# Issue order of the first transfers in a one-core hybrid decoder step: input tiles on two queues, parameters behind the first weight chunk

## The chip, the cores and the metric

The kernel runs on one core of a Trainium2 chip. The metric is the device time of one execution in microseconds (us); times of one kernel agree within a tenth of a us here. The core has a matmul engine (PE, TensorE, with its weight loads as PEld), VectorE (DVE), ScalarE (ACT), GpSimd (POOL) and a sync engine (SP), which only issues DMAs and waits. DMAs issued by SP go through one queue (q1 in the profile) and those issued by ACT through another (q10). Both are worked off by the same 16 DMA engines.

## What is computed

One decode step of one decoder layer for a prompt of 256 tokens and a sample group of 8 x 4 tokens, all f32, width 1024. The front of it, which is all that this case turns on:

```python
def rmsnorm(x, w):
    x32 = x.astype(jnp.float32)
    y = x32 * lax.rsqrt(jnp.mean(x32 * x32, axis=-1, keepdims=True) + EPS)
    return (y * w.astype(jnp.float32)).astype(x.dtype)
...
    xn = rmsnorm(x, norm1_w)
    proj = xn @ w_in
```

Behind it two branches (HGRN2 and RWKV-7) are run on the columns of `proj`, gated, merged and added to x; then comes a mixture of 32 experts, 4 for each token, whose weights (some 400 MB) are all read from memory; then a last RMSNorm. The small parameters of the RWKV-7 branch (`rwkv_mu`, `rwkv_w0`, `rwkv_a0`, `rwkv_k_k` and others) and of HGRN2 enter only after the first projection.

## The kernel before

The program is written out engine by engine, with semaphores; no scheduler reorders it, so the order of each engine's instructions is the order in the code.

**Start.** The 288 rows of x are three row tiles: tile 0 and tile 1 (128 rows of 4 KB each, 512 KB) of the prompt, tile 2 (32 rows) of the samples. SP issues, in this order: the norm weight (`norm1_w`, one row of 4 KB, into `norm_bc[0:1]`), the three row tiles into `xs`, the shift state (8 rows), chunk 0 of `w_in` (1 MB, as 1024 pieces of 1 KB), and four constants (`lora` twice, `g2`, `rb_bc`). Before chunk 1 it waits for `par_loaded`, that is, for all eleven parameter transfers; then it issues chunks 1 to 3, and each further chunk waits for PE to free its place in a ring of four.

ACT loads its function table, and issues the eleven parameter transfers: ten small ones into `par_rows` (14 or 4 rows of 512 B) and one of 128 rows (`gn_bc`). Then, for each row tile, it waits for `x_loaded{t}` and does a square with row sum (1.0 us), a logarithm and an exponential: that gives the tile's 1/rms (`rstd`).

PE waits for `ident` (POOL) and `norm_loaded`, and spreads the norm weight over 128 partitions by two matmuls of a row of ones with `norm_bc[0:1]`, into banks 6 and 7; their end is `par_T` 1. Then come `keep_busy(5)`, matmuls with no use for the result, and the transposes of the three tiles (8 each), each tile behind `xn_done`. `keep_busy(2)`, a wait for the five copies of the transposed tiles by ACT (`xT_evac`), and the projections follow: project(0) is the first matmul with chunk 0.

DVE waits for `par_T` 1, and for each tile for `rstd`; then it multiplies x by 1/rms and by the spread weight in banks 6 and 7, in two halves of 512 columns, and signals `xn_done`.

So the order of the start is: x tile to ACT, ACT to DVE, DVE to PE, PE to ACT, ACT to PE; and beside it norm weight to PE, PE to DVE.

**Afterwards.** The projections, the branches and the merge run until some 404 us. The experts follow, each with six transfers of 2 MB, issued by SP as soon as PE has used up what stood in a slot (`w_used`). The parameters are first used by one transpose on PE (`par_T` 2, line 589), behind the first eight k steps of project(0).

Of the kernel before, what the change touches and what calls it, by code (L numbers as in the profile page):

```python
# [27 lines left out]
P = 128  # L28
# [10 lines left out]
NP_, NS = 256, 32  # L39
# [3 lines left out]
TILES = [(0, 128), (128, 128), (256, 32)]  # L43
# [33 lines left out]
def layer_kernel(nc, x_prompt, x_sample, state_hgrn, state_rwkv, state_shift, norm1_w, w_in, hgrn_lb_logits,  # L77
# [5 lines left out]
    with ctx:  # L83
# [25 lines left out]
        gn_bc = take(128)  # L109
# [31 lines left out]
        xs = HR[:, 0:3 * D].rearrange("p (t d) -> p t d", t=3)  # L141
# [6 lines left out]
        par_rows = scratch[:, 11072 + 3 * D:11072 + 3 * D + 128]  # L148
# [93 lines left out]
        def S(name):  # L242
            if name not in names:
                names[name] = sem(name)
            return names[name]
# [147 lines left out]

        @block.sync
        def _(sp):
            sp.dma_start(norm_bc[0:1, :], norm1_w).then_inc(S("norm_loaded"), 16)
            for t, (o, n) in enumerate(TILES):
                src = x_prompt[0, o:o + n, :] if t < 2 else x_sample.rearrange("b t d -> (b t) d")
                sp.dma_start(xs[0:n, t, :], src).then_inc(S(f"x_loaded{t}"), 16)
            sp.dma_start(xn[NS:NS + NB, 2, :], state_shift[0]).then_inc(S("shift_loaded"), 16)  # L400
            for n in list(range(EARLY)) + [N_IN + 6, N_IN + 7] + list(range(EARLY, N_IN + 6)):
                if n == N_IN + 6:

                    sp.wait_ge(S("hg_state"), 8)
                    sp.wait_ge(S("hg_o_evac"), 3)
                    sp.wait_ge(S("rws_out"), 16 * NB)
                if n == N_IN + 4:
                    sp.wait_ge(S("rwp_out"), 16)
                    w_load(sp, 0, 2)
                    w_load(sp, 0, 3)  # L410
                if n == EARLY:
                    sp.wait_ge(S("hg_state"), 8)
                    sp.wait_ge(S("hg_o_evac"), 3)
                    w_load(sp, 0, 1)
                if n >= RING_MIX and n < N_IN + 6:
                    m = n - RING_MIX
                    if m < N_IN:
                        sp.wait_ge(S("pj_done"), pj_after(m))
                    else:
                        sp.wait_ge(S("branch"), 8)  # L420
                if n == 1:
                    sp.wait_ge(S("par_loaded"), 16 * 11)
                if n == 16:
                    sp.wait_ge(S("smp_pe"), smp_pe["scores"] + 2)
                if n == 20:
                    sp.wait_ge(S("smp_act"), smp_act["out"] + 4)
                    for b in range(NB):
                        src, dst = smp_state(S0T, rwkv_s, b)
                        sp.dma_start(dst, src).then_inc(S("rws_out"), 16)
                dst, src = mix_chunk(n)  # L430
                sp.dma_start(dst, src).then_inc(ring_loaded[n % RING_MIX] if n < N_IN + 6 else wo_loaded[n - N_IN - 6], 16)
                if n == 0:
                    sp.dma_start(lora[0:64, :], rwkv_w2[0]).then_inc(S("const_loaded"), 16)
                    sp.dma_start(lora[64:128, :], rwkv_a2[0]).then_inc(S("const_loaded"), 16)
                    sp.dma_start(g2, rwkv_g2[0]).then_inc(S("const_loaded"), 16)
                    sp.dma_start(rb_bc, router_b.partition_broadcast(P)).then_inc(S("const_loaded"), 16)
                if n == 6:
                    for b in range(NB):
                        dst, src = smp_state(S_s, state_rwkv, b)
                        sp.dma_start(dst, src).then_inc(S("s0_loaded"), 16)  # L440
                if n == 14:
                    sp.wait_ge(S("xT_done"), 5)
                    sp.wait_ge(S("shift_out"), 32)
                    sp.wait_ge(S("par_T"), 2)
                    sp.wait_ge(S("kn_done"), 1)
                    sp.dma_start(s0h.rearrange("p (b h v) -> p (b h) v", b=NB, h=HA), state_hgrn[0].rearrange("b h k v -> k (b h) v"))\
                      .then_inc(S("s0h_loaded"), 16)
                    w_load(sp, 1, 10)
# [29 lines left out]
            for n in range(FULL, PEELED + QUAD * ECH):  # L478
                b = before_chunk(n)
# [951 lines left out]
        def _(act):  # L1431
# [2 lines left out]

            nc.scalar.preload_act_table_set("natural_log_exp_and_others")

            r = 0
            for a in (rwkv_mu[0], rwkv_w0[0], rwkv_a0[0], rwkv_k_k[0], rwkv_k_a[0], None, hgrn_lb_logits[0], hgrn_lb_logits[1],
                      rwkv_ln_w[0], rwkv_ln_b[0]):
                src = rwkv_r_k[0].rearrange("(q h) n -> q (h n)", q=4) if a is None else a.rearrange("(r p) -> r p", p=P)  # L1440
                n = src.shape[0]
                act.dma_start(par_rows[r:r + n, :], src).then_inc(S("par_loaded"), 16)
                r += n
            act.dma_start(gn_bc, hgrn_gnorm_w.partition_broadcast(P)).then_inc(S("par_loaded"), 16)
            xv = xnT.rearrange("p (k t) -> p k t", k=KT)

            for t, (o, n) in enumerate(TILES):
# [1193 lines left out]
```

## Time and profile before

| | us |
|---|---|
| median of 3 executions (1316.35 to 1316.48) | 1316.41 |
| span of the profiled execution | 1314.0 |
| PE busy in that span | 1284.8 (98%) |
| first projection matmul starts at | 13.01 |

The span is what the profiler records from first to last instruction; 2.4 us of the device time lie around it. A timeline row gives the start, the time from there to the last end in the group, the engine, the line, the operation, the tile written and read, and how many instructions it merges; in brackets stands how long the engine was idle just before and what released it. PE's matmuls are pipelined: each record is longer than the distance to the next. "To landing" is the time from a DMA's issue until its semaphore says it is complete.

### The profile page before, as it was taken

What the parts mean: (1) busy time and instruction counts of PE and PEld (TensorE: products, weight loads), DVE (VectorE), ACT (ScalarE), POOL (GpSimd) and SP (SyncE); (2) the same over time, 40 slices, a digit from 0 to 9 for tenths busy, and PEclk for the clock granted to TensorE, in tenths of its full rate; (3) what the DMA queues carried; (4) which work ended last, traced back from release to release, by engine and by line L of the source; (5) the groups of instructions that cost most, each with busy time, mean ns of one, the idle gap of its engine ahead of it and who ended that gap; (6) DMA issues with size and microseconds to landing.
All of it is one profiled execution on the core that took longest, in us unless ns stands there. A gap on an engine that the chain in (4) does not pass through costs nothing.

```text
span 1314.0 us, 18370 instructions
## 1 busy us (share of the span) xinstructions
PE 1284.8 (98%) x7357; PEld 613.8 (47%) x7357; DVE 372.8 (28%) x1016; ACT 241.6 (18%) x532; POOL 56.6 (4%) x131
## 2 busy tenths in 40 slices
PE   9999999999999999999999999999999999999997
PEld 6778778888744333333333333333333333233333
DVE  3234756554327121121221211212112111211112
ACT  3144343222122110111111110111101101110102
POOL 5000200000060000000000000000000000000000
PEclk9999999999999999999999999999999999999999
DMA  7635437111879999999999999999999999999996
GB/s 237 172 98 192 134 81 274 36 34 34 307 279 379 428 429 428 428 428 428 430 428 428 427 430 431 430 429 429 429 429 431 430 430 430 429 429 430 430 429 265
DMA packets 73252, 449.40 MB, mean 342 GB/s; under 512 B 14408, under 2 KB 43130, under 8 KB 47884
## 3 DMA queue, kind: packets, MB, share of 16 engines
q1 hardware_dynamic: 67462, 445.45, 82.8%
q10 hardware_dynamic: 5734, 3.14, 0.8%
q8 instruction: 42, 0.69, 0.2%
q14 instruction: 14, 0.11, 0.0%
HBM read 443.82 MB, written 4.76 MB: 341 GB/s over the span
## 4 chain that ended last, share of the span: by engine, by line
PE 81%; DMA 14%; DVE 2%; ACT 2%; issue 0%; ACTq 0%; SPq 0%; DVEq 0%
PE bank L1288 26%; PE bank L1309 13%; DMA arena<-in_expert_w_gu_dram 7%; DMA ring<-in_expert_w_gu_dram 7%; PE bank L568 7%; PE bank L1203 5%; PE bank L658 5%; PE bank L1234 5%; PE bank L1082 2%; PE bank L1056 2%; PE bank L949 2%; ACT arena L1433 1%; PE bank L1210 1%; PE bank L1278 1%; PE bank L932 1%; PE bank L615 1%
## 5 line engine op out<-in xcount | busy, mean ns | idle before, releaser
L1288 PE MATMUL bank<-ring,arena 128*64 128x512 f32 x1040 | 233.6, 594 | 4.9 <-DMA ring<-in_expert_w_gu_dram 4.9
L1433 ACT ACTIVATE arena<-bank 128x512 f32<-128x512 f32 (+7 forms) x233 | 115.1, 514 | 479.2 <-PE bank L1309 196.2
L1288 PE MATMUL bank<-arena 128*64 128x512 f32 x768 | 173.3, 594 | 2.4 <-DMA arena<-in_expert_w_gu_dram 2.4
L1433 ACT ACTIVATE arena<-arena 128x256 f32<-128x256 f32 (+7 forms) x124 | 68.9, 564 | 468.9 <-DVE arena L2394 461.4
L1288 PEld LDWEIGHTS bank<-ring,arena 128*64 128x64 f32 x1040 | 72.8, 137 | 146.2 <-issue 122.8
L2394 DVE TENSOR_SCALAR arena<-bank 128x256 f32<-128x256 f32 x64 | 26.9, 421 | 375.5 <-PE bank L1288 375.5
L1309 PE MATMUL bank<-ring,arena 128*64 128x512 f32 x544 | 121.9, 595 | 0.0
L2440 DVE COPY arena<-bank 64x512 f32<-64x512 f32 x30 | 20.8, 693 | 318.5 <-PE bank L1309 318.5
L1288 PEld LDWEIGHTS bank<-arena 128*64 128x64 f32 x768 | 53.9, 137 | 105.8 <-issue 92.6
L1203 PE MATMUL bank<-arena 128*64 128x512 f32 x372 | 89.6, 599 | 0.0
L568 PE MATMUL bank<-arena,ring 128*128 128x296 f32 (+1 forms) x352 | 87.6, 411 | 0.0
L1309 PE MATMUL bank<-arena 128*64 128x512 f32 x352 | 79.8, 596 | 0.0
L568 PEld LDWEIGHTS bank<-arena,ring 128*128 128x128 f32 x352 | 66.7, 190 | 19.9
L658 PE MATMUL bank<-arena,ring 128*128 128x288 f32 x256 | 75.5, 419 | 0.0
L1309 PEld LDWEIGHTS bank<-ring,arena 128*64 128x64 f32 x544 | 37.8, 137 | 70.6 <-issue 69.3
L1234 PE MATMUL bank<-arena 128*32 128x256 f32 (+1 forms) x252 | 66.3, 491 | 0.0
L1288 PE MATMUL bank<-extra,arena 128*64 128x512 f32 x240 | 54.2, 593 | 0.7 <-DMA extra<-in_expert_w_gu_dram 0.7
L1203 PEld LDWEIGHTS bank<-arena 128*64 128x64 f32 x372 | 23.8, 134 | 60.6 <-issue 60.6
L1433 ACT ACTIVATE ring<-bank 128x512 f32<-128x512 f32 (+8 forms) x94 | 31.9, 382 | 95.1 <-PE bank L568 50.6
L658 PEld LDWEIGHTS bank<-arena,ring 128*128 128x128 f32 x256 | 44.0, 190 | 10.7 <-issue 2.4
L1309 PEld LDWEIGHTS bank<-arena 128*64 128x64 f32 x352 | 24.3, 137 | 45.2 <-issue 45.0
L1234 PEld LDWEIGHTS bank<-arena 128*32 128x32 f32 (+1 forms) x252 | 24.7, 148 | 34.4 <-issue 34.4
(374 smaller groups left out, 1127.0 us busy)
## 6 DMA issues: line engine op xcount, KB each, us to landing
ring<-in_expert_w_gu_dram SPq DMA_DIRECT2D x63, 2048.0 KB, 23.6
arena<-in_expert_w_gu_dram SPq DMA_DIRECT2D x47, 2048.0 KB, 23.0
ring<-in_expert_w_down_dram SPq DMA_DIRECT2D x35, 2048.0 KB, 23.6
arena<-in_expert_w_down_dram SPq DMA_DIRECT2D x21, 2048.0 KB, 24.6
extra<-in_expert_w_gu_dram SPq DMA_DIRECT2D x15, 2048.0 KB, 25.7
ring<-in_w_in_dram SPq DMA_DIRECT2D x23, 1024.0 KB, 5.2
extra<-in_expert_w_down_dram SPq DMA_DIRECT2D x6, 2048.0 KB, 25.6
ring<-in_w_out_dram SPq DMA_DIRECT2D x4, 1024.0 KB, 7.4
```

The costliest lines, as they stand in the source:

```text
L568: i = mm(b[:, 0:cols], slot[:, kt, j * P:(j + 1) * P], xv[:, kt, 0:cols], start=(kt == 0), stop=(kt == KT - 1))
L658: i = mm(bank[g % 2][:, 0:NT], slot[:, kt, (g % 2) * P:(g % 2 + 1) * P], xv[:, kt, 0:NT], start=(kt == 0), stop=(kt == KT - 1))
L949: i = mm(bank[6 - 4 * x][:, (hh % 2) * P:(hh % 2 + 1) * P], Pm, (zaT if lev > 3 else yaT)[:, hh * P:(hh + 1) * P], start=True, stop=True)
L1056: i = mm(bank[n % 2][:, 0:NT], slot[:, kt % 2, j * P:(j + 1) * P], (obT if br else oaT)[:, kt * NT:(kt + 1) * NT], start=(kt == 0), stop=( ...
L1082: i = mm(out, mT[:, kt * NT + o:kt * NT + o + rows], slot[:, kt % 2, c], start=(kt == 0), stop=True, skip_group_check=True)
L1203: i = mm(bank[6][64 * h:64 * h + 64, :], sel[0:rows, t * SLOTS:(t + 1) * SLOTS], x2[0:rows, t, h * 512:(h + 1) * 512], start=(t == 0), sto ...
L1234: return mm(out, GT[:, o:o + rows], yo[:, c], start=False, stop=True, skip_group_check=True)
L1288: ins = mm(bank[q % 2][64 * (q // 2):64 * (q // 2) + 64, :], gu_lhs(c), w[:, q * 512:(q + 1) * 512], start=(c == 0), stop=(c == KT - 1), s ...
L1309: ins = mm(b[64 * h:64 * h + 64, :], lhs(j, r), w[:, r * D + h * 512:r * D + (h + 1) * 512], start=(j == 0 and r == 0), stop=(j == DN - 1 ...
L1433: return nc.scalar.activation(out, in_, f, **kw)
L2394: v.tensor_scalar(by_row(glu, b), gu_half(b, 0), LIMIT, None, ALU.min).then_inc(S("glu_ready"), 1)
L2440: v.tensor_copy(yo[64 * x:64 * x + 64, 512:1024], bank[1][64:128, :]).then_inc(S("y_evac"), 1)
```

## The change

SP issues row tile 0 first, then the norm weight, the shift state and chunk 0; behind chunk 0 it issues the eleven parameter transfers, and then the four constants as before. ACT issues only row tiles 1 and 2. The waits are the same: SP still waits for all parameters ahead of chunk 1. No instruction of PE, DVE, POOL and no computing instruction of ACT is added, removed or moved.

```diff
         @block.sync
         def _(sp):
+            sp.dma_start(xs[:, 0, :], x_prompt[0, 0:P, :]).then_inc(S("x_loaded0"), 16)
             sp.dma_start(norm_bc[0:1, :], norm1_w).then_inc(S("norm_loaded"), 16)
-            for t, (o, n) in enumerate(TILES):
-                src = x_prompt[0, o:o + n, :] if t < 2 else x_sample.rearrange("b t d -> (b t) d")
-                sp.dma_start(xs[0:n, t, :], src).then_inc(S(f"x_loaded{t}"), 16)
             sp.dma_start(xn[NS:NS + NB, 2, :], state_shift[0]).then_inc(S("shift_loaded"), 16)
...
                 if n == 0:
+                    r = 0
+                    for a in (rwkv_mu[0], rwkv_w0[0], rwkv_a0[0], rwkv_k_k[0], rwkv_k_a[0], None, hgrn_lb_logits[0], hgrn_lb_logits[1],
+                              rwkv_ln_w[0], rwkv_ln_b[0]):
+                        src = rwkv_r_k[0].rearrange("(q h) n -> q (h n)", q=4) if a is None else a.rearrange("(r p) -> r p", p=P)
+                        sp.dma_start(par_rows[r:r + src.shape[0], :], src).then_inc(S("par_loaded"), 16)
+                        r += src.shape[0]
+                    sp.dma_start(gn_bc, hgrn_gnorm_w.partition_broadcast(P)).then_inc(S("par_loaded"), 16)
                     sp.dma_start(lora[0:64, :], rwkv_w2[0]).then_inc(S("const_loaded"), 16)
...
-            r = 0
-            for a in (rwkv_mu[0], rwkv_w0[0], rwkv_a0[0], rwkv_k_k[0], rwkv_k_a[0], None, hgrn_lb_logits[0], hgrn_lb_logits[1],
-                      rwkv_ln_w[0], rwkv_ln_b[0]):
-                src = rwkv_r_k[0].rearrange("(q h) n -> q (h n)", q=4) if a is None else a.rearrange("(r p) -> r p", p=P)
-                n = src.shape[0]
-                act.dma_start(par_rows[r:r + n, :], src).then_inc(S("par_loaded"), 16)
-                r += n
-            act.dma_start(gn_bc, hgrn_gnorm_w.partition_broadcast(P)).then_inc(S("par_loaded"), 16)
+            act.dma_start(xs[:, 1, :], x_prompt[0, P:NP_, :]).then_inc(S("x_loaded1"), 16)
+            act.dma_start(xs[0:NS, 2, :], x_sample.rearrange("b t d -> (b t) d")).then_inc(S("x_loaded2"), 16)
```

Sync engine, from its first transfer on, before (a row is line, kind, destination<-source, shape):

```order
L396 DMA arena<-in_norm_w_dram 1x1024
L399 DMA ring<-in_x_prompt_dram 128x1024 x2
L399 DMA ring<-in_x_sample_dram 32x1024
L400 DMA ring<-in_state_shift_dram 8x1024
L431 DMA ring<-in_w_in_dram 128x8x256
L433 DMA arena<-in_rwkv_w_dram 64x512
```

and after:

```order
L396 DMA ring<-in_x_prompt_dram 128x1024
L397 DMA arena<-in_norm_w_dram 1x1024
L398 DMA ring<-in_state_shift_dram 8x1024
L429 DMA ring<-in_w_in_dram 128x8x256
L435 DMA ring<-in_rwkv_mu_dram 14x128
L435 DMA ring<-in_rwkv_w_dram 4x128
...
L437 DMA arena<-in_hgrn_gnorm_w_dram 128x128
L438 DMA arena<-in_rwkv_w_dram 64x512
```

The norm weight has one tile of 512 KB ahead of it in its queue where it had nothing, and eleven transfers stand between chunk 0 and the constants.

ScalarE, from its start to the first square, before:

```order
L1435 ACT_TABLE_LOAD
L1442 DMA ring<-in_rwkv_mu_dram 14x128
L1442 DMA ring<-in_rwkv_w_dram 4x128
...
L1442 DMA ring<-in_rwkv_ln_b_dram 4x128
L1444 DMA arena<-in_hgrn_gnorm_w_dram 128x128
L1433 ACTIVATE ring,arena<-ring 128x1024
```

and after:

```order
L1440 ACT_TABLE_LOAD
L1442 DMA ring<-in_x_prompt_dram 128x1024
L1443 DMA ring<-in_x_sample_dram 32x1024
L1438 ACTIVATE ring,arena<-ring 128x1024
L1438 ACTIVATE arena<-arena,epsc 128x1
```

Two issues instead of eleven stand ahead of the first square.

## Rows read from the trace of the kernel before

**Rows 1.** The page: span, and PE's busy time with its share.

```profile
span 1314.0 us, 18370 instructions
...
PE 1284.8 (98%) x7357; PEld 613.8 (47%) x7357; DVE 372.8 (28%) x1016; ACT 241.6 (18%) x532; POOL 56.6 (4%) x131
```

**Rows 2.** Table of stretches: busy us (xinstructions) of each engine, granted clock, DMA share, GB/s.

```profile
0.00:13.00 13.00, 10.09 (x42) 6.97 (x42) 4.20 (x6) 8.35 (x18) 9.19 (x53) 1.00 0.78 224
13.00:404.00 391.00, 388.12 (x3091) 296.17 (x3089) 181.24 (x407) 116.54 (x284) 42.72 (x70) 1.00 0.48 161
404.00:932.00 528.00, 526.84 (x2516) 184.28 (x2514) 115.59 (x375) 67.38 (x130) 1.82 (x7) 1.00 1.00 426
932.00:1290.00 358.00, 342.69 (x1603) 116.88 (x1605) 66.00 (x218) 42.41 (x82) 0.00 (x0) 1.00 1.01 430
```

**Rows 3.** Timeline of the first 14 us, ScalarE and its queue (ACTq).

```profile
0.82 0.65 ACTq L1442 DMA_DIRECT2D ring<-in_rwkv_mu_dram  x1
1.50 0.27 ACTq L1442 DMA_DIRECT2D ring<-in_rwkv_w_dram  x1
...
4.73 0.55 ACTq L1444 DMA_DIRECT2D arena<-in_hgrn_gnorm_w_dram  x1
5.33 1.06 ACT L1433 ACTIVATE ring<-ring 128x1024 f32<-128x1024 f32 x1 [3.26 <-DMA ring<-in_x_prompt_dram]
...
10.04 0.20 ACT L1433 ACTIVATE arena<-arena 32x1 f32<-32x1 f32 x1
...
12.52 0.44 ACT L1433 ACTIVATE arena<-bank 128x320 f32<-128x320 f32 x1 [0.37 <-PE bank L558]
```

**Rows 4.** Timeline of the same stretch, VectorE: first and last row tile.

```profile
7.16 1.41 DVE L1920 SCALAR_TENSOR_TENSOR ring<-ring,arena,bank 128x512 f32<-128x512 f32 x2 [7.16 <-ACT arena L1433]
...
10.34 1.39 DVE L1920 SCALAR_TENSOR_TENSOR ring<-ring,arena,bank 32x512 f32<-32x512 f32 x2 [0.20 <-ACT arena L1433]
```

**Rows 5.** Timeline of the same stretch, TensorE.

```profile
2.50 3.75 PE L541 MATMUL bank<-arena 1*128 1x512 f32 x4 [2.50 <-DMA arena<-in_norm_w_dram]
6.17 2.50 PE L547 MATMUL bank<-arena 128*128 128x128 f32 x10
8.62 2.76 PE L558 MATMUL bank<-arena,ring 128*128 128x128 f32 x16
11.79 0.69 PE L558 MATMUL bank<-arena,ring 40*128 40x40 f32 x8 [0.41 <-DVE ring L1920]
...
13.01 4.25 PE L568 MATMUL bank<-arena,ring 128*128 128x296 f32 x16
17.19 0.26 PE L589 MATMUL bank<-arena,ring 50*128 50x50 f32 x1
```

**Rows 6.** Timeline of the same stretch, the sync engine's issues (SPq).

```profile
0.79 0.36 SPq L396 DMA_DIRECT2D arena<-in_norm_w_dram  x1
1.21 0.84 SPq L399 DMA_DIRECT2D ring<-in_x_prompt_dram  x2
...
2.97 0.41 SPq L431 DMA_DIRECT2D ring<-in_w_in_dram  x1
```

**Rows 7.** DMA view by issue: tile 0 (issued at 1.21), tile 1 (1.6), chunk 0; last number us to landing.

```profile
ring<-in_x_prompt_dram SPq DMA_DIRECT2D x1, 512.0 KB, 3.5
...
ring<-in_x_prompt_dram SPq DMA_DIRECT2D x1, 512.0 KB, 5.1
...
ring<-in_w_in_dram SPq DMA_DIRECT2D x1, 1024.0 KB, 8.3
```

**Rows 8.** DMA view, packets by queue: 1.7 to 2.1 us, 2.1 to 3.7, 3.7 to 4.1.

```profile
q10 hardware_dynamic: 28, 0.01, 7.6%
...
q1 hardware_dynamic: 110, 0.45, 86.5%
...
q1 hardware_dynamic: 45, 0.14, 96.3%
q10 hardware_dynamic: 5, 0.00, 9.1%
```

**Rows 9.** Waits of the sync engine, first 60 us: total us, times, longest.

```profile
SPq L431 <- DMA arena<-in_hgrn_gnorm_w_dram: 6.6, 1, 6.6
```

## The prediction, on record before the changed kernel ran

> **What bounds the kernel now.** I read the page first: PE is busy for 1284.8 of 1314.0 us [rows 1]. Then the table of stretches [rows 2]: up to 404 us PE is all but always busy and the DMA engines are at half load; from 404 to 932 both are full; from 932 on the DMA engines are at 1.01 with 430 GB/s while PE has gaps (342.69 of 358). So the middle belongs to PE and the end to the stream of expert weights. The change touches neither. It can only move the moment at which PE's unbroken work begins, and whatever it moves there is passed on: nearly all of PE's idle time in the front lies before 13.01, and the weight stream of the end is issued against what PE has used, so it starts later when PE is later. I take the shift at 13.01 us as the shift of the whole.
>
> The second thing to read is therefore the first 13 us, by engine. There are two strands.
>
> **The x strand.** ACT issues parameters until 4.73 + 0.55 = 5.28 and squares tile 0 at 5.33 [rows 3]. Tile 0 had landed at 1.21 + 3.5 = 4.7 [rows 6, 7], so although the row names the DMA as releaser, the issues were the later of the two, by 0.6 us. From there ACT needs 1.6 us a tile; the last 1/rms ends at 10.04 + 0.20, DVE starts tile 2 at 10.34 for 1.39 [rows 4], PE transposes it at 11.79 for 0.69 [rows 5], ACT copies at 12.52 for 0.44 [rows 3], and project(0) starts at 13.01 [rows 5]. That strand is 13.01 - 5.33 = 7.68 us from first square to first projection, and now it is the one that sets the start.
>
> **The norm strand.** PE begins to spread the norm weight at 2.50, released by its landing, and needs until 6.25; keep_busy follows from 6.17 to 8.67, and the transposes start at 8.62 [rows 5]. DVE could not start before 6.25 either, since it multiplies by the spread weight; it started at 7.16, so this strand had 0.9 us of slack on DVE, but on PE, behind keep_busy, almost none: the transposes began when keep_busy ended.
>
> **What the change gives on the x strand.** Tile 0 is issued at 0.79 instead of 1.21: landing at 0.79 + 3.5 = 4.3 if nothing disturbs it. ACT has only two issues, done by some 0.82 + 0.65 + 0.27 = 1.8 (row tiles may cost the 0.42 each that SP paid), far earlier. First square at 4.35: 0.98 us gained, projection at 4.35 + 7.68 = 12.03 by this strand. If tile 1 on the other queue halves tile 0's rate, tile 0 lands up to 1.3 us later (the time of tile 1's packets, below), 5.6, and the strand ends at 13.3. Tile 1 is wanted 1.6 us after tile 0, tile 2 3.2 after; neither binds.
>
> **What it costs on the norm strand.** The norm weight is issued second, 0.42 us later. That alone would be N = 2.92 for its landing. But it is one row of 4 KB, and in its queue 128 rows of tile 0 are now ahead of it. Is a later transfer held up by an earlier one? In one queue the landings keep the order of issue: tile 0 at 4.7, tile 1 at 1.6 + 5.1 = 6.7, chunk 0 at 2.97 + 8.3 = 11.3 [rows 6, 7]. Across queues: ACT's first transfer (14 rows) went through at 1.7 to 2.1, 28 packets, before tile 0 filled the engines; `rwkv_w0`, issued at 1.50, should have followed about a us behind its issue, but from 2.1 to 3.7 the ACT queue has no packet at all, 110 are SP's, and ACT's next 5 come at 3.7 to 4.1, when tile 0's 128 are through [rows 3, 8]. So an engine serves tile 0's whole share before it turns to the other queue. Applied to the change: tile 0's share, then ACT's turn, which is tile 1's share, and only then the norm weight. I take that. In packets: tile 0 starts some 1.0 us after its issue (as the first packets did, issue 0.79 to 0.82, packets from 1.7), at 1.75; 110 of the 256 packets of both tiles in 1.6 us, the other 146 at 45 in 0.4 us, that is 1.3 us: 4.65. The weight's own packet (0.2) and what stood between its packet and its use before (seen by 1.9, used at 2.50: 0.6 to 0.8) give **N = 5.55, say 5.6**. Bounds: directly behind tile 0, N = 4.3 to 4.5; behind the full landing of tile 1, which was 2.0 us after tile 0's, 4.3 + 2.0 + 0.2 = 6.5.
>
> The Trainium skill has the same picture in the page DMA: Bandwidth & Descriptors, section Queues, rings and completion order: each engine takes turns between queues a whole packet at a time, with typically 9 to 17 descriptors in one. The ACT queue's silence from 2.1 to 3.7 agrees with that. Its section Issuing engines are not separate DMA queues speaks against this change: a second issuing engine saves only the issuing time. By it the x strand's gain is the issue time alone, which is what the sum has.
>
> From N on, PE works in one chain: 6.0 us to the end of keep_busy (8.62 - 2.50, less the 0.1 that DVE held it), both full tiles' transposes 2.76, tile 2's 0.69, copy and release 13.01 - 12.48 = 0.53: 9.98, less 0.1 to 0.2 because pipelined groups overlap, as 8.67 and 8.62 do. I use **9.85** [rows 5]. DVE beside it: from N + 3.75 three tiles of 1.41 and small gaps end at N + 8.2, so tile 2 is ready when PE comes to it (N + 8.7). DVE's second strand is hidden by PE's keep_busy, and PE's is the late one. The granted clock reads 1.00 throughout [rows 2], 2.4 GHz, yet ten 128-column matmuls took 2.50 and 16 transposes of the same width 2.76, so PE was faster at the end of this stretch than at its start, after it had worked for a while. If it is fast from the first transpose on, 0.9 comes off; if slow to the end, up to 1.3 comes on. I keep the pattern, counted from N.
>
> Sum: projection starts at 5.6 + 9.85 = 15.45 instead of 13.01: **+2.4 us**. The x strand (12.0 to 13.3) is then under cover.
>
> **The other parts cost nothing.** Chunk 0 is issued 1 us earlier (0.79 + 3 x 0.41 instead of 2.97) behind the same bytes: it lands by 11.3 or so, and is wanted at 15.4. The eleven parameters, at 0.32 to 0.65 each [rows 3], keep SP at it for some 4.5 us, and the constants for 2.6 behind them: to 9.5. Before, SP waited until 12.65 anyway, 6.6 us for the parameters [rows 9]. Now they follow chunk 0 in the queue and land at 12 or so. Chunk 1 is thus issued about when it was; it needs 5 to 6 us and is wanted at 15.4 + 8 = 23. The parameters' transpose (17.19) is behind PE's own work. All this has 2 us or more of cover; were it gone, chunk 1 would hold PE only if it were issued after 17.
>
> The span of the profile is 1314.0 and lies 2.4 below the median of 1316.41; the shift is added to the median: 1316.41 + 2.4 = **1318.8**. About 0.2%, 2.63 us, is what a measurement of this kernel can tell from no change; the forecast is just inside.
>
> **Rivals.**
> A. The norm weight is not held up (it overtakes, or its engine is free): N = 2.92, PE's chain gives 12.77, the x strand 12.03, so -0.2: 1316.2. This is the case in which it is not slower. For it: the weight is one packet on one engine. Against it: landings in issue order. Note that even then the gain is capped by PE's chain, not by the x tile. 0.13.
> B. The weight follows tile 0 directly (SP's queue served ahead of ACT's): N = 4.4, 14.25, +1.2: 1317.7. For it: SP issues 0.03 us earlier and its first issue took 0.36 where ACT's took 0.65. 0.20.
> C. It waits for all of tile 1, slow engines too: N = 6.5, 16.35, +3.3: 1319.8. It decides from N = 5.79 on (13.01 + 2.63 - 9.85), which is where +0.2% begins. For it: tile 1's landing trailed tile 0's by 2.0 us. 0.28.
> D. The shift is lost on the way, because the weight stream at the end is bound by memory and started early enough: 1316.4. Against it: the DMA engines are at half load up to 404 us [rows 2], since the slots come free by PE. 0.04.
> Forecast, N from 5.0 to 5.79: 0.33. Faster by more than 0.2% would need 2.6 of the 13 us, which no strand offers: 0.02.
>
> **How the numbers follow.** Slower by over 0.2% is C, 0.28; faster 0.02; within 0.2% are A, B, D and the forecast, 0.70. The range leaves out A, D and the top of C: 1316.9 to 1319.8.
>
> **What would show it.** In the changed kernel's trace: the first L546 matmul (the former 541) released by the norm weight at 5.6 instead of 2.50; the first square at about 4.35; DVE's first product waiting for PE, not for ACT; transposes from 11.6; the first projection at 15.4; from there every row later by the same amount. I am wrong if the first matmul of the norm weight starts before 4, if PE waits for chunk 0 or 1, or if the shift at 15 us is not found at 404 and at the end.

## The result and the profile after

The changed kernel is slower: 1319.68 us against 1316.0 (9 executions each), ratio 1.0033 with a 95% interval of 1.0022 to 1.0044. The prediction was 1318.8, inside the bound of 0.2%; the measured time lies in the range of 1316.9 to 1319.8, but on the other side of the bound, in rival C. In about one execution in five (47 of 237, from none of eleven to four of five by kernel) the granted clock was lower for about 10 us (0.994 to 0.997 over the whole instead of 0.998 or 0.999), mostly near 400 us, which costs 4 to 5 us, and the "undisturbed" medians below leave out these and three far longer executions of the kernel before. For the changed kernel that is 1319.3 against 1316.0, or +0.25%, still outside the bound.

Two statements of the opening need a correction. Times of one kernel do not agree within a tenth of a us: undisturbed executions of the kernel before lie between 1315.1 and 1316.8, and its median was 1316.41 in the first three executions and 1316.0 in the nine here. And some 1.75 us, not 2.4, lie around the span where time and span are of the same execution (1319.32 and 1317.6 here); 2.4 compared a median with the span of another one. The forecast used only the shift, +2.4, so neither changes it; the measured shift is +3.3.

The page of the changed kernel, answering [rows 1]:

```profile
span 1317.6 us, 18370 instructions
...
PE 1284.6 (97%) x7357; PEld 613.7 (47%) x7357; DVE 372.5 (28%) x1016; ACT 241.8 (18%) x532; POOL 56.4 (4%) x131
```

The same work, 3.6 us longer. The stretches of [rows 2], moved by 2 or 3 us, in the changed kernel (same columns):

```profile
0.00:15.00 15.00, 8.85 (x34) 6.16 (x35) 4.21 (x6) 7.63 (x17) 10.67 (x60) 1.00 0.76 206
15.00:407.00 392.00, 389.10 (x3100) 296.99 (x3098) 180.92 (x407) 117.44 (x287) 41.10 (x62) 1.00 0.49 160
407.00:935.00 528.00, 526.85 (x2516) 184.25 (x2514) 115.58 (x375) 67.37 (x130) 1.83 (x7) 1.00 1.00 426
```

Only the first row tells a difference: in 15 us PE was busy for 8.85, where 10.09 of 13 had been. Timeline of the start in the changed kernel, answering [rows 3, 4, 5, 6]: issues and ScalarE first,

```profile
0.79 0.40 SPq L396 DMA_DIRECT2D ring<-in_x_prompt_dram  x1
0.81 0.40 ACTq L1442 DMA_DIRECT2D ring<-in_x_prompt_dram  x1
...
1.25 0.32 SPq L397 DMA_DIRECT2D arena<-in_norm_w_dram  x1
...
5.97 1.06 ACT L1438 ACTIVATE ring<-ring 128x1024 f32<-128x1024 f32 x1 [3.91 <-DMA ring<-in_x_prompt_dram]
```

then PE and DVE:

```profile
6.15 3.75 PE L546 MATMUL bank<-arena 1*128 1x512 f32 x4 [6.15 <-DMA arena<-in_norm_w_dram]
...
9.83 2.50 PE L552 MATMUL bank<-arena 128*128 128x128 f32 x10
9.94 4.28 DVE L1919 SCALAR_TENSOR_TENSOR ring<-ring,arena,bank 128x512 f32<-128x512 f32 x6 [9.94 <-PE bank L546]
...
12.13 3.29 PE L563 MATMUL bank<-arena,ring 128*128 128x128 f32 x24
...
15.95 4.25 PE L573 MATMUL bank<-arena,ring 128*128 128x296 f32 x16
```

The norm weight's landing releases PE at 6.15 instead of 2.50. Everything behind it is one unbroken chain to the first projection at 15.95, instead of 13.01: +2.94. DVE was released by ACT before; it now waits for PE. And the first square begins at 5.97, not earlier than before but 0.64 later, although ACT had done issuing at 1.7. The reason stands in the DMA view of the changed kernel, tile 0 (SP) and tile 1 (ACT), then the packets of 4.1 to 4.3 us by queue, answering [rows 7, 8]:

```profile
ring<-in_x_prompt_dram SPq DMA_DIRECT2D x1, 512.0 KB, 5.2
ring<-in_x_prompt_dram ACTq DMA_DIRECT2D x1, 512.0 KB, 5.7
...
q10 hardware_dynamic: 10, 0.04, 50.1%
q1 hardware_dynamic: 10, 0.04, 49.7%
```

Ten packets of each queue in 0.2 us, and ten or eleven in each 0.2 us from 3.7 to 4.9: the two tiles are carried side by side, each at half speed. Tile 0 takes 5.2 us to land instead of 3.5.

Whether the shift is passed on: SP's issues of weights near 400 us, first of the kernel before,

```profile
391.85 6.42 SPq L323 DMA_DIRECT2D ring<-in_expert_w_gu_dram  x3
401.25 0.33 SPq L323 DMA_DIRECT2D arena<-in_expert_w_gu_dram  x1
```

and of the changed kernel:

```profile
394.86 6.42 SPq L323 DMA_DIRECT2D ring<-in_expert_w_gu_dram  x3
404.26 0.33 SPq L323 DMA_DIRECT2D arena<-in_expert_w_gu_dram  x1
```

3.01 us, both times. The chain of waits (start us, us, what) enters its memory-bound part with the same distance, in the kernel before and in the changed one:

```profile
939.33 28.81 DMA ring<-in_expert_w_gu_dram
```

```profile
942.34 29.42 DMA ring<-in_expert_w_gu_dram
```

There 0.6 us come on top. Undisturbed executions of one and the same kernel differ by that much and more, and in a second profile of the changed kernel, below, this part is missing; so I don't explain it by the change.

### The profile page after: what moved, and what is told of

The parts are those of the page before. It is cut to its first block, busy times and chain, and to the rows that moved or that the text cites. A ratio compares the mean times of both kernels' runs of the same rounds, so it can differ in the third digit from the quotient of the medians.

```text
span 1317.6 us, 18370 instructions
## 1 busy us (share of the span) xinstructions
PE 1284.6 (97%) x7357; PEld 613.7 (47%) x7357; DVE 372.5 (28%) x1016; ACT 241.8 (18%) x532; POOL 56.4 (4%) x131
## 3 DMA queue, kind: packets, MB, share of 16 engines
HBM read 443.82 MB, written 4.76 MB: 340 GB/s over the span
## 4 chain that ended last, share of the span: by engine, by line
PE 81%; DMA 15%; DVE 2%; ACT 1%; issue 0%; SPq 0%; DVEq 0%; ACTq 0%
PE bank L1293 26%; PE bank L1314 13%; DMA arena<-in_expert_w_gu_dram 7%; DMA ring<-in_expert_w_gu_dram 7%; PE bank L573 7%; PE bank L1208 5%; PE bank L663 5%; PE bank L1239 5%; PE bank L1087 2%; PE bank L1061 2%; PE bank L954 2%; ACT arena L1438 1%; PE bank L1215 1%; PE bank L1283 1%; PE bank L937 1%; PE bank L620 1%
## 5 line engine op out<-in xcount | busy, mean ns | idle before, releaser
L663 PEld LDWEIGHTS bank<-arena,ring 128*128 128x128 f32 x256 | 44.0, 190 | 10.8 <-issue 2.4
```

The lines of the kernel that those rows point to most:

```text
L663: i = mm(bank[g % 2][:, 0:NT], slot[:, kt, (g % 2) * P:(g % 2 + 1) * P], xv[:, kt, 0:NT], start=(kt == 0), stop=(kt == KT - 1))
```

## The experiments

Undisturbed medians, and the difference to the kernel before as it ran beside them (1316.03, 1315.95 and 1315.68 in three sets). The ratio, with its 95% interval, is not over the undisturbed ones alone. N is when PE starts on the norm weight, P the first projection, both of the profiled execution. In params_only, params_only_again and norm_first PE was released at N not by the weight but by the identity matrix that POOL builds (the rows name `POOL arena`): the weight was there before, so 2.3 to 2.4 is a floor of N and not the weight's own time.

| kernel | N | P | median (executions) | to before | ratio |
|---|---|---|---|---|---|
| before | 2.50 | 13.01 | 1316.03 (25) | | |
| changed | 6.15 | 15.95 | 1319.27 (6) | +3.3 | 1.0033 (1.0022 to 1.0044) |
| after_again | 6.67 | 16.40 | 1319.15 (11) | +3.5 | 1.0023 (1.0014 to 1.0032) |
| order_only | 4.61 | 14.60 | 1317.35 (11) | +1.7 | 1.0011 (1.0000 to 1.0022) |
| tiles_only | 6.71 | 17.43 | 1319.46 (7) | +3.8 | 1.0028 (1.0015 to 1.0042) |
| params_only | 2.38 | 12.81 | 1315.35 (10) | -0.7 | 0.9997 (0.9985 to 1.0009) |
| params_only_again | 2.30 | 12.66 | 1316.01 (10) | +0.3 | 1.0002 (0.9990 to 1.0014) |
| norm_after_chunk0 | 10.14 | 20.96 | 1322.40 (6) | +6.4 | 1.0052 (1.0035 to 1.0069) |
| x1_late | 4.42 | 19.83 | 1322.54 (1 of 5) | +6.5 | 1.0068 (1.0045 to 1.0090) |
| norm_first | 2.38 | 16.23 | 1319.61 (8) | +3.6 | 1.0026 (1.0013 to 1.0039) |
| norm_first_filled | 2.95 | 15.03 | 1317.64 (9) | +1.7 | 1.0004 (0.9990 to 1.0018) |
| norm_by_act | 3.21 | 13.99 | 1315.73 (9) | -0.3 | 0.9994 (0.9982 to 1.0007) |
| halves | 2.52 | 15.95 | 1319.70 (10) | +3.7 | 1.0017 (1.0002 to 1.0031) |
| after_no_warmup | 6.27 | 16.28 | 1321.18 (6) | +5.2 | 1.0037 (1.0023 to 1.0052) |

My theory (Q) was that the norm weight, behind the tiles in the queue, holds PE's chain, P = N + 9.8. Its main rival (X) was that tile 0, slowed by tile 1, is to blame.

**order_only**: the kernel before, with the norm weight one place later.

```diff
-            sp.dma_start(norm_bc[0:1, :], norm1_w).then_inc(S("norm_loaded"), 16)
             sp.dma_start(xs[:, 0, :], x_prompt[0, 0:P, :]).then_inc(S("x_loaded0"), 16)
+            sp.dma_start(norm_bc[0:1, :], norm1_w).then_inc(S("norm_loaded"), 16)
             sp.dma_start(xs[:, 1, :], x_prompt[0, P:NP_, :]).then_inc(S("x_loaded1"), 16)
```

> The kernel before with one swap on SP: tile 0 first, then the norm weight; tiles 1 and 2 stay on SP behind it, the parameters on ACT. Theory Q (the weight is held up by what is ahead of it in its own queue): N = 4.4 to 4.6, as when tile 1 was issued late; norm strand N + 9.8 = 14.3; x strand 13.0 as before. First projection at 14.3, span 1315.3, clean times 1317.3. So of the 2.94 us of the whole change 1.3 belong to the place behind tile 0. Rival W (all of it belongs to sharing with the second queue): N near 2.9, projection 13.0, span 1314.0.

Timeline of order_only, PE:

```profile
4.61 3.75 PE L541 MATMUL bank<-arena 1*128 1x512 f32 x4 [4.61 <-DMA arena<-in_norm_w_dram]
...
14.60 4.25 PE L568 MATMUL bank<-arena,ring 128*128 128x296 f32 x16
```

N came where Q says, P 0.3 us later: one swap of two issues, with both tiles on SP's queue, costs 1.7 us. The interval of the ratio begins at 1.0000, but the trace agrees: P is 1.59 us later, and SP's first issue near 400 us 1.62 (393.47 against 391.85). N went up by 2.1 with one tile ahead in the queue.

**tiles_only**: the changed kernel's tiles, with the parameters left on ACT behind tiles 1 and 2.

```diff
+            act.dma_start(xs[:, 1, :], x_prompt[0, P:NP_, :]).then_inc(S("x_loaded1"), 16)
+            act.dma_start(xs[0:NS, 2, :], x_sample.rearrange("b t d -> (b t) d")).then_inc(S("x_loaded2"), 16)
             r = 0
             for a in (rwkv_mu[0], rwkv_w0[0], rwkv_a0[0], rwkv_k_k[0], rwkv_k_a[0], None, hgrn_lb_logits[0], hgrn_lb_logits[1],
```

> The other half of the change: SP issues tile 0, norm weight, shift and chunk 0 as in the changed kernel, ACT issues tiles 1 and 2 and behind them the eleven parameters, which thus stay on ACT. Theory Q: the parameters' place doesn't matter, N = 6.1, norm strand 15.9; ACT is through with issuing at 6.1 and starts the squares then, x strand 13.8. First projection at 15.9, span 1317.3 to 1317.7, the same as the changed kernel. Rival P (the parameters on SP carry part of the loss, by chunk 1 or by traffic): span 0.5 or more below the changed kernel's.

Timeline of tiles_only, PE:

```profile
6.71 3.75 PE L539 MATMUL bank<-arena 1*128 1x512 f32 x4 [6.71 <-DMA arena<-in_norm_w_dram]
...
17.43 3.76 PE L566 MATMUL bank<-arena,ring 128*128 128x296 f32 x14
```

It costs as much as the whole change (+3.8 against +3.5), so the loss is in the tiles and the norm weight, and rival P is out. P came at N + 10.7: the 24 transposes took 4.22 us instead of 3.29, with no gap before or between them, and why PE's pace rose later here no run shows. The step from order_only to here, N from 4.6 to 6.7, comes with tiles 1 and 2 on the other queue.

**params_only**: the other half alone; and the same kernel once more.

```diff
+            sp.dma_start(xs[:, 1, :], x_prompt[0, P:NP_, :]).then_inc(S("x_loaded1"), 16)
+            sp.dma_start(xs[0:NS, 2, :], x_sample.rearrange("b t d -> (b t) d")).then_inc(S("x_loaded2"), 16)
...
-            act.dma_start(xs[:, 1, :], x_prompt[0, P:NP_, :]).then_inc(S("x_loaded1"), 16)
-            act.dma_start(xs[0:NS, 2, :], x_sample.rearrange("b t d -> (b t) d")).then_inc(S("x_loaded2"), 16)
```

(a diff to the changed kernel, in which the norm weight also stands ahead of tile 0 again)

> Only the second half of the change: parameters issued by SP behind chunk 0, while SP issues norm weight, tile 0, 1 and 2 as in the kernel before, and ACT issues nothing at the start. Theory Q: N = 2.5, norm strand 12.3; tile 0 lands at 4.7, x strand 12.4; first projection at 12.4 to 12.5, 0.55 us earlier than before, span 1313.4. Rival P (moving the parameters behind chunk 0 costs time itself, by a late chunk 1 or a late parameter transpose): the gap on PE appears at chunk 1 (some 21 us) or at the parameter transpose, and the span is 1314 or more.

Timeline of params_only, ACT's first two squares and the first projection:

```profile
4.76 1.06 ACT L1440 ACTIVATE ring<-ring 128x1024 f32<-128x1024 f32 x1 [2.69 <-DMA ring<-in_x_prompt_dram]
...
6.72 1.06 ACT L1440 ACTIVATE ring<-ring 128x1024 f32<-128x1024 f32 x1 [0.25 <-DMA ring<-in_x_prompt_dram]
...
12.81 4.25 PE L575 MATMUL bank<-arena,ring 128*128 128x296 f32 x16
```

ACT, free of issuing, squares tile 0 at 4.76 instead of 5.33, but must then wait for tile 1, which lands at 6.7 as ever: of 0.57 us won, 0.2 reach P. Chunk 1 and the parameters hold nobody.

> params_only once more, for a second set of times beside a new set of the kernel before: if its gain of some 0.6 us (1315.35 against 1316.03) is real, the medians of the undisturbed times differ by 0.4 to 0.9 again; if it was chance, by less than 0.2.

The first time the undisturbed median was 0.7 below the kernel before, the second time 0.3 above, and both intervals of the ratio hold 1. By what I had set down, a gain of 0.4 to 0.9 was not found again. P is 0.2 to 0.35 earlier in both profiles; the time cannot tell it from no change.

**x1_late**: ACT waits for tile 0 before it issues tiles 1 and 2.

```diff
+            act.wait_ge(S("x_loaded0"), 16)
             act.dma_start(xs[:, 1, :], x_prompt[0, P:NP_, :]).then_inc(S("x_loaded1"), 16)
```

> The changed kernel, but ACT waits until tile 0 has landed before it issues tiles 1 and 2; so tile 0 and the norm weight have the engines alone. It splits the delay of N into what tile 0 ahead in the queue costs and what tile 1's sharing costs. Theory Q: N falls from 6.15 to 4.5 (tile 0 at 4.3, weight right behind it), norm strand 14.3; tile 1 lands near 8.3 and the x strand gives 8.3 + 6.1 = 14.4: projection at 14.4, span 1315.4 to 1316. Rival X: N stays near 6.

Timeline of x1_late:

```profile
4.42 3.75 PE L546 MATMUL bank<-arena 1*128 1x512 f32 x4 [4.42 <-DMA arena<-in_norm_w_dram]
...
12.65 1.06 ACT L1438 ACTIVATE ring<-ring 128x1024 f32<-128x1024 f32 x1 [5.32 <-DMA ring<-in_x_prompt_dram]
```

and three rows of its table of stretches (the third number from the end is the granted clock):

```profile
13.00:14.00 1.00, 0.00 (x0) 0.00 (x0) 0.00 (x0) 0.97 (x3) 0.73 (x5) 1.00 0.19 64
...
20.00:21.00 1.00, 1.00 (x4) 0.69 (x3) 0.00 (x0) 0.00 (x0) 0.73 (x5) 0.50 1.11 348
...
23.00:24.00 1.00, 1.00 (x6) 0.76 (x5) 0.00 (x0) 0.00 (x0) 0.86 (x3) 1.00 0.71 227
```

N fell from 6.15 to 4.42, as Q said: without tile 1 beside it, the weight lands right behind tile 0. The rest of my expectation was wrong: tile 1, issued at 4.70, landed only at 12.6, for chunk 0 was by then being carried in the other queue. P came at 19.83 instead of 14.4, behind a gap of 3.61 us on PE. Here the profile also shows the granted clock fall, to 0.50 (the 1.2 GHz level) from 15.6 to 22.5 us; PE had stood still since 12.3, and began again at 15.9. The first sixteen projections took 5.46 us. The time is thus no measure of the sharing; it shows what a tile costs that is issued behind a chunk, and the clock that PE loses by waiting for it.

**norm_after_chunk0**: the norm weight behind the first weight chunk.

```diff
-            sp.dma_start(norm_bc[0:1, :], norm1_w).then_inc(S("norm_loaded"), 16)
...
                 if n == 0:
+                    sp.dma_start(norm_bc[0:1, :], norm1_w).then_inc(S("norm_loaded"), 16)
                     r = 0
```

> A dose: the changed kernel with the norm weight issued one place later still, behind chunk 0 (1 MB). Theory Q (what stands ahead in the queue holds the weight up, and the first projection starts at N + 9.8): the weight lands with chunk 0, N = 10.4 to 10.7, first projection at 20.3, 4.4 us later than in the changed kernel and 7.3 later than before; passed on in full: span 1321.4 to 1322. Rival X: N stays at 6.15, because the weight is a single packet that finds a gap; span 1317.6.

Timeline of norm_after_chunk0, PE:

```profile
10.14 3.75 PE L546 MATMUL bank<-arena 1*128 1x512 f32 x4 [10.14 <-DMA arena<-in_norm_w_dram]
```

The dose works in its direction: 4 KB wait for 1 MB to go through, N = 10.14, and the median is 6.4 above the kernel before and 3.1 above the changed one. It does not come out in full. P rose by 5.0 from the changed kernel and by 7.95 from the kernel before (the transposes took 4.32 us, with no gap), and at 400 us the profiled execution is 8.0 later (399.86 against 391.85), yet the undisturbed spans, 1319.9 to 1320.9, lie below the 1321.4 that I expected. The profiled execution was the longest of the ten; whether the others started their projections sooner, no profile shows.

**norm_first**: the changed kernel with the norm weight ahead of tile 0.

```diff
-            sp.dma_start(xs[:, 0, :], x_prompt[0, 0:P, :]).then_inc(S("x_loaded0"), 16)
             sp.dma_start(norm_bc[0:1, :], norm1_w).then_inc(S("norm_loaded"), 16)
+            sp.dma_start(xs[:, 0, :], x_prompt[0, 0:P, :]).then_inc(S("x_loaded0"), 16)
```

> The changed kernel with one swap: SP issues the norm weight ahead of row tile 0. Theory Q (the norm weight queues behind the tiles, and PE's chain from its landing N sets the start of the first projection at N + 9.8): N is 2.5 again, so the norm strand gives 12.3; tile 0, issued at 1.2 and sharing the engines with tile 1, lands near 6.4 and the x strand then sets the start, 6.4 + 7.7 = 14.1, 1.1 us later than in the kernel before: span about 1315.1, time ratio 1.001. Rival X (the delay comes from tile 0 landing late under tile 1, the norm weight's place doesn't matter): no better than the changed kernel, projection at 15.9 or later, span 1317.6.

DMA view of norm_first: tile 1, issued by ACT at 0.82, and tile 0, issued by SP at 1.21:

```profile
ring<-in_x_prompt_dram ACTq DMA_DIRECT2D x1, 512.0 KB, 3.7
...
ring<-in_x_prompt_dram SPq DMA_DIRECT2D x1, 512.0 KB, 6.1
```

and its timeline, ACT and PE:

```profile
6.06 2.50 PE L552 MATMUL bank<-arena 128*128 128x128 f32 x10
7.31 1.06 ACT L1438 ACTIVATE ring<-ring 128x1024 f32<-128x1024 f32 x1 [5.24 <-DMA ring<-in_x_prompt_dram]
...
10.60 4.68 PE L563 MATMUL bank<-arena,ring 128*128 128x128 f32 x24 [2.04 <-DVE ring L1919]
...
16.23 5.85 PE L573 MATMUL bank<-arena,ring 128*128 128x296 f32 x16
```

Neither theory holds as a whole. N is back at 2.38, so Q's queue is right and X's "its place doesn't matter" is wrong; yet the kernel is no faster than the changed one, as X had forecast. First, the tile that is wanted last went first: 0.4 us of head start let tile 1 land after 3.7 us, and tile 0 took 6.1. The packets of norm_first from 2.1 to 3.3 us show it, and no packet of SP's queue is among them:

```profile
DMA packets 71, 0.29 MB, mean 242 GB/s; under 512 B 0, under 2 KB 0, under 8 KB 71
...
q10 hardware_dynamic: 71, 0.29, 76.5%
```

Second, PE, idle for 2.0 us ahead of the transposes, did them in 4.68 us instead of 3.29 and the first sixteen projections in 5.85 instead of 4.25, although the granted clock reads 1.00 (the 2.4 GHz level) in that stretch. P came 1.2 later than the x strand's 7.31 + 7.68 = 15.0, and another 1.6 us were lost behind P: near 400 us SP issues 4.83 us later than before (396.68), which is P's 3.22 and these 1.6. The eight undisturbed times spread from 1317.6 to 1321.0, with the profiled one at the upper end, so the pace was not lost to this extent in all of them. That gave a new theory (G): PE has to be kept at work through the start, and keep_busy(5) does that only if x comes in time.

**norm_first_filled** tests G: the same, with more idle work for PE.

```diff
-            keep_busy(5, bank[5])
+            keep_busy(12, bank[5])
```

> norm_first with keep_busy(12) instead of keep_busy(5): the only addition is matmuls without use, which fill PE's wait for tile 0. Theory G (in norm_first PE's pace stayed at 0.49 us a 296-column matmul, against 0.25, until 20 us because PE had been idle for 2.0 us ahead of the transposes): with the gap filled the transposes and the first projection run at full pace; the x strand sets the start, 7.3 + 7.7 = 15.0; first projection's 16 matmuls take 4.25 instead of 5.85; span 1316.0 to 1316.6 against 1319.2. Rival T (the pace rises when it will, filled or not): the projection starts at 16.2 or later, for more work stands ahead of it, and the span is 1319 or more.

Timeline of norm_first_filled, PE:

```profile
6.63 5.48 PE L552 MATMUL bank<-arena 128*128 128x128 f32 x24
...
15.03 4.25 PE L573 MATMUL bank<-arena,ring 128*128 128x296 f32 x16
```

Seven more turns of keep_busy (fourteen matmuls in the profile) make it 2.0 us faster (1317.64 against 1319.61; all nine undisturbed times lie between 1316.4 and 1318.1, five of norm_first's eight above 1319); P and the sixteen matmuls are as G says. Chance is unlikely, though the two intervals of the ratio still touch. **after_no_warmup** is the reverse:

```diff
-            keep_busy(5, bank[5])
```

> The changed kernel without keep_busy(5), whose 2.5 us stood ahead of the transposes. Theory G (PE needs to be without a gap to come to full pace, and loses more by a gap than keep_busy costs): PE waits for DVE from 9.9 to 11.4, transposes and part of the first projections run at half pace; first projection at 15.5 to 16.5 and its 16 matmuls take over 4.25; span 1318 or more, no better than 1317.6. Rival K (keep_busy was merely in the way, so that PE's chain was 0.9 us longer than DVE's): first projection at 15.0, span 1316.7.

Timeline of after_no_warmup, PE:

```profile
11.51 4.24 PE L562 MATMUL bank<-arena,ring 128*128 128x128 f32 x24 [1.50 <-DVE ring L1918]
...
16.28 4.25 PE L572 MATMUL bank<-arena,ring 128*128 128x296 f32 x16
```

In the profiled execution the projections ran at full pace, against G, and its span was 1317.2. But that execution was one of the two fastest: the six undisturbed ones lie at 1318.9 (twice) and from 1320.9 to 1321.5, a median 1.9 above the changed kernel. Rival K, which wanted a first projection at 15.0 and a span of 1316.7, is out. That leaving keep_busy out costs 2 us is only suggested: it rests on four executions, the ratio of the table is 1.0037 against the changed kernel's 1.0033, and how the pace rose in the slower executions no profile shows.

**norm_by_act**: the weight on a queue of its own.

```diff
-            sp.dma_start(norm_bc[0:1, :], norm1_w).then_inc(S("norm_loaded"), 16)
+            sp.dma_start(xs[:, 1, :], x_prompt[0, P:NP_, :]).then_inc(S("x_loaded1"), 16)
+            sp.dma_start(xs[0:NS, 2, :], x_sample.rearrange("b t d -> (b t) d")).then_inc(S("x_loaded2"), 16)
...
-            act.dma_start(xs[:, 1, :], x_prompt[0, P:NP_, :]).then_inc(S("x_loaded1"), 16)
-            act.dma_start(xs[0:NS, 2, :], x_sample.rearrange("b t d -> (b t) d")).then_inc(S("x_loaded2"), 16)
+            act.dma_start(norm_bc[0:1, :], norm1_w).then_inc(S("norm_loaded"), 16)
```

> SP issues tile 0 first, then 1, 2, shift, chunk 0, parameters; ACT issues only the norm weight, on its own queue, at 0.8. Theory Q: the norm weight has nothing ahead of it in its queue, N = 2.5, and tile 0 is undisturbed and lands at 4.3: norm strand 12.3, x strand 12.0, first projection at 12.3, span 1313.3, 0.7 us better than before. Rival S (what holds the weight up is the load on the engines, whatever the queue): N between 3.5 and 5, projection at 13.3 to 14.8, span 1314.3 to 1315.8.

Timeline of norm_by_act, PE:

```profile
3.21 3.75 PE L547 MATMUL bank<-arena 1*128 1x512 f32 x4 [3.21 <-DMA arena<-in_norm_w_dram]
...
13.99 4.25 PE L574 MATMUL bank<-arena,ring 128*128 128x296 f32 x16
```

Between the two theories, which wanted 2.5 and 3.5 to 5: N = 3.21, better than behind a tile (4.61), worse than ahead of everything (2.50 where the weight sets it). The other queue is no free lane either; whether tile 0, issued 0.02 us sooner, or ACT's longer issue (0.54 us) holds the weight up, no run separates. P came at N + 10.8, by the same later rise of pace as in tiles_only. The median is 0.3 below the kernel before: no difference that can be told.

**halves**: each full tile split between the queues, so that both work on tile 0 first.

```diff
-            sp.dma_start(xs[:, 0, :], x_prompt[0, 0:P, :]).then_inc(S("x_loaded0"), 16)
-            sp.dma_start(xs[:, 1, :], x_prompt[0, P:NP_, :]).then_inc(S("x_loaded1"), 16)
+            sp.dma_start(xs[0:64, 0, :], x_prompt[0, 0:64, :]).then_inc(S("x_loaded0"), 16)
+            sp.dma_start(xs[0:64, 1, :], x_prompt[0, P:P + 64, :]).then_inc(S("x_loaded1"), 16)
...
+            act.dma_start(xs[64:P, 0, :], x_prompt[0, 64:P, :]).then_inc(S("x_loaded0"), 16)
+            act.dma_start(xs[64:P, 1, :], x_prompt[0, P + 64:NP_, :]).then_inc(S("x_loaded1"), 16)
```

> Made from params_only: the norm weight is SP's first transfer, and each full row tile is split, rows 0 to 63 by SP and 64 to 127 by ACT, tile 2 by ACT; both queues work on tile 0 first. What each theory expects: Theory Q: N = 2.4, norm strand 12.2; tile 0 whole at 4.3 to 4.7, tile 1 at 5.9 to 6.3, x strand 12.0 to 12.4: first projection 12.2 to 12.4, span 1313.0, 0.4 below params_only (12.8, held by tile 1 at 6.7). Rival H (two queues at once make both halves of tile 0 late, as in the changed kernel, where tile 0 took 5.2 us instead of 3.5): tile 0 at 5.5 or later, projection 13.2 or later, span 1314 or more.

Timeline of halves, ACT's two squares and the first projection:

```profile
5.55 1.06 ACT L1439 ACTIVATE ring<-ring 128x1024 f32<-128x1024 f32 x1 [3.48 <-DMA ring<-in_x_prompt_dram]
...
8.76 1.06 ACT L1439 ACTIVATE ring<-ring 128x1024 f32<-128x1024 f32 x1 [1.49 <-DMA ring<-in_x_prompt_dram]
...
15.95 5.99 PE L574 MATMUL bank<-arena,ring 128*128 128x296 f32 x16
```

Tile 0 is whole at 5.5 instead of 4.7, tile 1 at 8.7 instead of 6.7, and the gap of 1.22 us on PE that follows slows the projections too (5.99 for sixteen). These are rival H's numbers, but its reason, two queues at once, is not what the packets show. From 3.7 to 4.3 us only SP's queue moves data, from 4.5 to 5.1 all but only ACT's, and in both the engines are full at little more than half the rate. First halves from 3.7 to 4.3, then the changed kernel from 3.3 to 4.9:

```profile
DMA packets 35, 0.14 MB, mean 239 GB/s; under 512 B 0, under 2 KB 0, under 8 KB 35
...
q1 hardware_dynamic: 35, 0.14, 103.0%
```

```profile
DMA packets 162, 0.66 MB, mean 415 GB/s; under 512 B 0, under 2 KB 0, under 8 KB 162
```

From these numbers a row of 4 KB kept an engine busy for 0.28 us in halves and for 0.16 in the changed kernel; the transfer had 64 rows instead of 128. So halves changes the height of a transfer along with the split, and its loss can't be put down to two queues at once.

**after_again**: the changed kernel, a second time.

> The changed kernel itself, on the same chip and beside the same runs of the kernel before. Theory Q gives 2.9 us from the start plus what the first profile shows in the weight stream (0.7), so 3.0 to 3.6 between the medians; and N again at 6.0 to 6.3, first projection at N + 9.8.

Timeline of after_again, PE:

```profile
6.67 3.75 PE L546 MATMUL bank<-arena 1*128 1x512 f32 x4 [6.67 <-DMA arena<-in_norm_w_dram]
...
16.40 4.25 PE L573 MATMUL bank<-arena,ring 128*128 128x296 f32 x16
```

N is 0.5 later than in the first profile and 0.4 above what I had expected; P = N + 9.73. The shift of P is 3.39, and the span, 1317.3, is 3.3 above that of the kernel before: here it is passed on one to one, and nothing is added at the end.

## Why the prediction was off

**What held.** The norm strand became the late one; PE's chain behind the weight was taken at 9.85 and measured 9.80 and 9.73; the shift at P is found again at 400 us (3.01 for 2.94). The moved parameters cost nothing: SP waited 3.5 us for them instead of the 6.6 of [rows 9],

```profile
SPq L429 <- DMA arena<-in_hgrn_gnorm_w_dram: 3.5, 1, 3.5
```

issued chunk 1 at 12.75 instead of 12.65, and neither chunk 1 nor the parameter transpose (20.13) held PE.

**The step that failed** is the term N, at "N = 5.55, say 5.6". It measured 6.15 and 6.67. With 9.8 behind it this is the difference between +2.4 and +2.9 to +3.4, and it carries the result over the bound, which lay at N = 5.79. The mechanism, a weight held up by the tiles ahead of it, is right; its size is not. Two things in that step were wrong.

The first is the reading of [rows 8]. From ACT's queue being silent between 2.1 and 3.7 I concluded that an engine serves the whole share of tile 0 before it turns to the other queue. That does happen, with full tiles too, where one has a head start: in norm_first, issued 0.39 us ahead, tile 1 alone was carried from 2.1 to 3.3. In the kernel before tile 0 was 0.29 us ahead of `rwkv_w0`. In the changed kernel the two tiles are issued 0.02 us apart, and there the queues share, ten to ten. I carried a reading from the one case over to the other; what decides between them inside an engine no run shows. For the norm weight this makes little difference, by the forecast's own count, as tile 1 is ahead of it either way; for tile 0 it makes 1.7 us (5.2 instead of 3.5), so the gain that I gave the x strand, 0.98 us, was not there: first square at 5.97, forecast 4.35. The recorded alternative, a tile 0 at half rate that lands at 5.6, was the nearer one. The page DMA: Bandwidth & Descriptors of the Trainium skill, section Issuing engines are not separate DMA queues, says that transfers of several issuing engines interleave on the same engines; this trace agrees, with 10 and 10 packets in 0.2 us, while norm_first has 1.2 us in which they do not.

The second is the rate. I counted 110 packets for the first 1.6 us and then 112 in a us: both tiles through at 4.65. The 45 packets that gave the 112 were not all rows of 4 KB: the row has 0.14 MB for them, where 45 such rows would be 0.18. By bytes the other 146 rows take 1.7 us instead of 1.3, which is 0.4 of the 0.55 us that N was late. In the changed kernel tile 0's last packets run until about 5.0 and tile 1's on beyond that, 20 in 0.2 us at best, and PE was released some 1.1 us behind the last packets of tile 0, where I had given 0.9 behind the last of both tiles.

**The chances** were off in the same way. I put 0.33 on N from 5.0 to 5.79 and 0.28 on more, with a bound of 6.5 taken from tile 1's landing. That the time fell into C's stretch does not show C's reason, a weight that waits for all of tile 1: in the first profile PE was released at 6.15 and tile 1 landed at 6.5, in the second at 6.67 and 6.5. The row that says what a full landing takes (1.6 + 5.1 = 6.7, [rows 6, 7]) was nearer to the case than my count of packets, because it has the tail in it that a count leaves out.

**Where the 3.3 to 3.5 us come from**, by the runs: 1.7 for the weight's place behind one tile (order_only), some 1.8 more with tiles 1 and 2 on the other queue (after_again), and nothing or a few tenths either way for the parameters (params_only, and tiles_only against after_again). Open is the part beyond PE's shift: 0.7 in the first profile, none in the second.

**A better version** was not found. params_only starts the projections 0.2 to 0.35 us earlier, norm_by_act 1.0 later in its profile, and their times can't be told from the kernel before.

## What to carry to other kernels

A small transfer on which an engine's first work hangs goes ahead of every large one, in its own queue above all: behind 512 KB its 4 KB came 2.1 us later, behind two tiles 3.7 to 4.2. Two large transfers issued at the same time from two engines both land late; if one is wanted first, give it a head start (0.39 us was enough here), but not so long that a larger transfer gets between (x1_late). An issue saved on one engine (ACT's eleven here) is worth only what the next transfer's landing leaves. When the start of a kernel moves, look also at whether PE still has work without a gap: here filling a wait with matmuls for nothing gave back 2.0 us.

## What the runs showed of the hardware that I had not expected

- 0.39 us of head start on another queue decides the order of two equal transfers: tile 1 issued at 0.82 landed after 3.7 us, tile 0 issued at 1.21 after 6.1. Issued 0.02 us apart they took 5.2 and 5.7.
- A tile (512 KB in rows of 4 KB) issued while a chunk in pieces of 1 KB was being carried by the other queue took 7.9 us, against 3.5 (kernel before) and 3.9 (x1_late) for tile 0 with no large transfer beside it.
- With all engines busy, a transfer of 64 rows of 4 KB went at 239 GB/s, two of 128 rows at 415 (halves, changed kernel).
- The profile can show a granted clock of 0.50: in x1_late, behind 3.6 us without work on PE, it lasted some 7 us.
- In the first 20 us PE's pace is not what the granted clock says. With 1.00 granted throughout, sixteen projections took 4.25 us where PE had worked since the norm weight with no gap over 0.5 us, and 5.85 and 5.99 where it had stood still for 1.2 to 2.0 us before or between the transposes (norm_first, halves), about as slow as x1_late's 5.46, where the profile does show 0.50; the profiled execution of after_no_warmup, with 1.5 us of gap and 4.25, was the exception. Even without a gap the pace rose at different times: P came between N + 9.7 and N + 10.8.
